# One-core transformer block kernel: vector sums reordered inside the block pairs of the up product, a four-pair TensorE loop, two down tiles computed by half contractions

## What is computed

```python
D_FF = 3 * D_MODEL                       # 3072
h = rms_norm(x, g_ffn_pre)
up = h @ w_up                            # (1024, 6144)
gate_h = causal_dwconv(up[..., :D_FF], ffn_conv_w, ffn_conv_b)   # 3 taps over tokens
hid = jax.nn.gelu(gate_h) * up[..., D_FF:]
x = x + rms_norm(hid @ w_down, g_ffn_post)
```

## Time and profile before

| | us |
|---|---|
| median of three runs | 3272.5 (3272.47 to 3274.01) |
| the profiled execution, its own time | 3272.96 |
| its span, first to last instruction | 3271.2 |
| PE busy in it | 3088.3 (94%) |
| DVE busy in it | 2314.0 (71%) |

### The profile page before, as it was taken

How to read it: one execution, slowest core, us unless ns; L and a number is a source line. 1 busy time by engine, 2 the same in 40 slices (tenths; PEclk the granted TensorE clock), 3 DMA queues, 4 the chain that set the end, 5 groups by cost and what they waited for, 6 DMA issues and landing times.

```text
span 3271.2 us, 44920 instructions
## 1 busy us (share of the span) xinstructions
PE 3088.3 (94%) x14885; PEld 2455.6 (75%) x14885; DVE 2314.0 (71%) x2995; ACT 1473.5 (45%) x2003; POOL 981.6 (30%) x511
## 2 busy tenths in 40 slices
PE   6999998888998799999969999999989999999998
PEld 5668776566786688888857888888767777778867
DVE  7788967886545899999966775633588888811266
ACT  4345433667222788888841366201443343300142
POOL 2224342000341011111104433345234444434432
PEclk8999999999998899999989999999999999999999
DMA  7223221340242999999972222134133333454312
GB/s 263 71 63 93 65 65 52 110 120 30 81 160 85 378 382 379 380 382 382 352 267 60 64 83 87 41 120 145 64 91 104 114 103 108 155 206 148 115 33 71
DMA packets 365271, 496.54 MB, mean 152 GB/s; under 512 B 34478, under 2 KB 237148, under 8 KB 365156
## 3 DMA queue, kind: packets, MB, share of 16 engines
q1 hardware_dynamic: 350356, 460.39, 41.0%
q10 hardware_dynamic: 5440, 17.86, 1.7%
q0 software_dynamic: 9360, 16.80, 1.4%
HBM read 422.57 MB, written 83.92 MB: 155 GB/s over the span
## 4 chain that ended last, share of the span: by engine, by line
PE 43%; DVE 13%; issue 4%; SPq 3%; DMA 2%; ACT 2%; DVEq 0%; POOL 0%; ACTq 0%; POOLq 0%
PE acc L450 9%; PE acc L451 9%; PE acc L452 9%; PE acc L2049 3%; PE acc L2051 3%; PE acc L2050 3%; DVE TT L3064 3%; PE acc L2068 1%; PE acc L2070 1%; PE acc L2069 1%; DVE UWL L2817 1%; SPq L1952 1%; DVE uu L3070 1%; DVE TT L3073 1%; DMA mraw<-in_exp_w 1%
## 5 line engine op out<-in xcount | busy, mean ns | idle before, releaser
L421 POOL TENSOR_TENSOR whi<-wraw,one 128x1024 fp32r<-128x1024 f32 (+1 forms) x153 | 289.9, 1895 | 1312.2 <-PE acc L452 1014.4
L450 PE MATMUL acc<-Ah,whi 128*128 128x512 f32 (+1 forms) x1568 | 620.3, 396 | 4.6 <-POOL wlo L423 3.2
L452 PE MATMUL acc<-Ah,wlo 128*128 128x512 f32 (+1 forms) x1568 | 611.0, 390 | 0.0
L451 PE MATMUL acc<-Al,whi 128*128 128x512 f32 (+1 forms) x1568 | 611.0, 390 | 0.0
L423 POOL TENSOR_TENSOR wlo<-wraw,whi 128x1024 fp32r<-128x1024 f32 (+1 forms) x153 | 381.5, 2493 | 12.0
L450 PEld LDWEIGHTS acc<-Ah,whi 128*128 128x128 f32 (+1 forms) x1568 | 294.2, 188 | 81.5 <-issue 18.9
L451 PEld LDWEIGHTS acc<-Al,whi 128*128 128x128 f32 (+1 forms) x1568 | 294.4, 188 | 63.6 <-issue 3.1
L452 PEld LDWEIGHTS acc<-Ah,wlo 128*128 128x128 f32 (+1 forms) x1568 | 294.2, 188 | 62.6
L2162 DVE TENSOR_TENSOR mlo<-mraw,mhi 128x1024 fp32r<-128x1024 f32 x256 | 306.9, 1222 | 37.5 <-ACT mhi L2106 23.8
L2106 ACT ACTIVATE mhi<-mraw 128x1024 fp32r<-128x1024 f32 x256 | 267.8, 1063 | 74.5 <-PE acc L2051 51.6
L2049 PE MATMUL acc<-mhi,XTh 128*128 128x512 f32 x512 | 203.8, 398 | 3.6 <-DVE XTl L2157 3.3
(11 more groups left out here) (726 smaller groups left out, 6651.0 us busy)
## 6 DMA issues: line engine op xcount, KB each, us to landing
mraw<-in_exp_w SPq DMA_DIRECT2D x512, 256.0 KB
mraw<-in_exp_w SPq DMA_DIRECT2D x128, 512.0 KB, 12.1
wraw<-in_w_in SPq DMA_DIRECT2D x72, 512.0 KB, 3.8
TT<-in_ada_w SPq DMA_DIRECT2D x32, 512.0 KB, 3.8
TT<-gates SPq DMA_DIRECT2D x32, 512.0 KB, 4.6
wraw<-in_w_up SPq DMA_DIRECT2D x24, 512.0 KB, 4.7
hidTh<-hidh SPq DMA_DIRECT2D x24, 512.0 KB, 2.6
hidTl<-TT SPq DMA_DIRECT2D x24, 512.0 KB, 3.6
```

Source lines behind the costliest of these rows:

```text
L421: ch(pool.tensor_tensor(hi[:, r, 0:k, 0:m], wraw[:, r, 0:k, 0:m], one[:, 0:1].unsqueeze(2).broadcast_to([P, k, m]), ALU.mult))
L450: pe.matmul(o, hi[:, hr, j, 0:m], ih[:, k0 + j, cols], start=(j == 0), stop=False)
L451: pe.matmul(o, hi[:, hr, j, 0:m], il[:, k0 + j, cols], start=False, stop=False)
L452: last = pe.matmul(o, lo[:, hr, j, 0:m], ih[:, k0 + j, cols], start=False, stop=(j == k - 1))
```

## The change

It has four edits. (1) In the loop and in pair 22, DVE does `result_e` ahead of the low part of weight 0, `result_f` ahead of that of weight 1, and `result_22` ahead of step 2. (2) Around pair 1, the first three sums of pair 1 stand between the readings of the second plain pair's banks, and the rest of the plain pairs' hidden tiles (step 2 of tile 0, the convolution of tile 1) behind them; the third sum goes to `uf` in place and is copied to `uu` later; step 2 of tile 1 goes to the end. On ACT `conv_first(1)` stands ahead of `hidden_high(0)`. (3) PE's loop holds four pairs and runs five times. (4) The two down tiles are computed in the order tile 0 with k = 0 to 3, tile 1 with k = 0 to 3, tile 0 with k = 4 to 7, tile 1 with k = 4 to 7, and the wait for the second tile's weights and bank stands in front of the second tile.

```diff
@@ ACT
+        conv_first(act, 1, 0, 32)
         hidden_high(act, 0, 1)
-        conv_first(act, 1, 0, 32)
         gelu(act, 1, 0)
@@ DVE, around pair 1
         weight_low(dve, 1, 5, 1, True)
-        second_half(0, 1, 2)
...
         dve.wait_ge(S("t_lo"), 16)
+        result_e(1, 1)
         ch(dve.tensor_tensor(ug[:], XX[:], R5, ALU.mult))
         dve.sem_inc(S("ug"), 1)
-        result_e(1, 1)
+        result_f(1, 1)
         ch(dve.tensor_tensor(uu[:], Y[:], R5, ALU.mult))
         dve.sem_inc(S("up_done"), 1)
+        dve.wait_ge(S("u_mid"), 3 + 2)
+        dve.wait_ge(S("u_used"), 7 + 4)
+        dve.tensor_tensor(uf[:], UBANKS[1][3], uf[:], ALU.add).then_inc(S("u_mid"), 1)
+        second_half(0, 1, 2)
         conv(1, 0)
-        result_f(1, 1)
         weight_low(dve, 2, 0, 0)
         second_half(1, 0, 1)
-        result_22(1, 1)
+        dve.wait_ge(S("u_mid"), 3 + 3)
+        ch(dve.tensor_copy(uu[:, hi_tok], uf[:]))
         for i in (1, 2):
             weight_low(dve, 2, i, 0)
-        second_half(1, 0, 2)
         result_11(1, 1)
...
         result_21(1, 1)
+        second_half(1, 0, 2)
@@ DVE, pair(n, p)
             conv(n, 1 - p)
+            result_e(n, p)
             if weights:
                 weight_low(dve, n + 1, 0, 1 - p)
-            result_e(n, p)
+            result_f(n, p)
             if weights:
                 weight_low(dve, n + 1, 1, 1 - p)
             second_half(n, 1 - p, 1)
-            result_f(n, p)
             if weights:
                 weight_low(dve, n + 1, 2, 1 - p)
+            result_22(n, p)
             second_half(n, 1 - p, 2)
-            result_22(n, p)
@@ PE
-        with pe.Fori(0, (BLOCKS - 2) // 2) as i:
+        with pe.Fori(0, (BLOCKS - 2) // 4) as i:
+            for r in range(4):
+                pair(4 * i + 2 + r, r % 2)
...
     def product_two(pe, n, ih, il):
+        for part in range(2):
             for r in range(2):
+                if part == 0:
+                    pe.wait_ge(w_lo, n + r + 1)
+                    pe.wait_ge(acc_free[r], take(r))
+                for j in range(4 * part, 4 * part + 4):
+                    if j % 2 == 0:
+                        pe.wait_ge(S(f"hid_in0_{j // 2}"), 64)
...
```

More of the change, by code:

```diff
@@ L3308, in _ @@
         pair(1, 1, tuple(("t_lo", 4 * q) for q in range(4)))
-        with pe.Fori(0, (BLOCKS - 2) // 2) as i:
-            for r in range(2):
-                pair(2 * i + 2 + r, r)
+        with pe.Fori(0, (BLOCKS - 2) // 4) as i:
+            for r in range(4):
+                pair(4 * i + 2 + r, r % 2)
         pair(BLOCKS, 0)
     def product_two(pe, n, ih, il):
[L3316 to L3321, removed]
-            for r in range(2):
[L3323 to L3328, removed]
+        for part in range(2):
+            for r in range(2):
+                if part == 0:
[4 more added lines that the diff above has]
+                        pe.wait_ge(S(f"hid_in0_{j // 2}"), 64)
+                    for h in range(2):
+                        o = acc[r][:, tokens(h)]
+                        pe.matmul(o, whi[:, r, j, :], ih[:, j, tokens(h)], start=(j == 0), stop=False)
+                        pe.matmul(o, whi[:, r, j, :], il[:, j, tokens(h)], start=False, stop=False)
+                        last = pe.matmul(o, wlo[:, r, j, :], ih[:, j, tokens(h)], start=False, stop=(j == KD - 1))
+                if part:
                     last.then_inc(w_used, 1)
```

## The result

Six executions of the changed kernel took 3302.84 us in the median (3299.74 to 3304.21), against 3274.02 us (3272.47 to 3276.75, six runs) for the kernel before on the same chip: a ratio of 1.0086, 95% interval 1.0074 to 1.0098, or 28 us slower. The median lies 15 us above the forecast of 3287.5 us and just beyond the upper end of the range; 1.5 us of that is the kernel before itself, which came out at 3274.0 in these six runs and at 3272.5 in the three from which the forecast started.

The account below looks back on a forecast made before the run. DVE was taken to pace the loop, with PE following. The terms +4.5 + 13.0 - 1.1 - 1.6 = +14.8 on 3272.96 gave 3287.8, stated as 3287.5 us since the median is 0.5 lower; range 3275 to 3302.

Parts of the forecast that it names:

- What bounds the kernel: In the loop of block pairs DVE sets the pace and PE follows, with 0.73 us a pair to spare.
- The order, 20 x 0.65 = +13.0: Loop pairs 2 to 21: the second sum, free in the gap before, costs DVE 0.65 us a pair, +13.0 in all.
- two effects oppose: In the pairs: the first sum hides a POOL operation, while POOL, released earlier, meets DVE's SBUF-only instructions; net 0.
- one meeting of 0.78: In the pairs: each overlap of POOL's work with DVE's taps or low parts costs DVE about 0.78 us.
- Shorter taps and low parts: Sign in the loop: the forecast is wrong if DVE's taps or low parts get shorter.
- POOL takes more: Rival in the loop: one more POOL meeting in each pair, 1.4 us a pair, 3302; chance 0.19.
- Behind the gap, third sum and step 2 only change places: In each pair, behind the gap after step 1: this swap was given no cost to DVE.
- The start, +4.5: Around pair 1: later step 2 of tile 0 delays SP's store and pair 2's weights; DVE enters the loop 4.5 late.
- The end of the loop, -1.1: At pair 22, which goes at PE's pace: the third sum comes earlier for part 6, -1.1 once.
- The down tiles, -1.6: Down product: PE starts 1.3 us earlier, stalls inside tile 0, no wait ahead of tile 2; -1.6.
- PE's longer loop, 0: PE's loop of four pairs: PE's spacing unchanged and PE has spare time anyway, so 0.
- my fourth rival: PE's longer loop stalls: an instruction fetch at each of four jumps back, up to +8, 3295; chance 0.05.

Follow-up runs that it names:

- third_early: The kernel before with only the third sum moved ahead of step 2 in the pairs; 3275.13 us, ratio 1.0004.
- second_early: The kernel before with only the second sum moved ahead of step 1 in the pairs; 3287.44 us, ratio 1.0037.
- order_only: The kernel before with only the new order of DVE's sums in the loop and in pair 22; 3300.84 us, ratio 1.0078.
- third_late: order_only with the third sum alone put back behind step 2; 3277.17 us, ratio 1.0008 to the kernel before.
- second_third: The kernel before with the second sum ahead of step 1 and the third ahead of step 2, first sum unmoved; 3305.50 us, ratio 1.0094.
- start_only: The kernel before with only the edits around pair 1, DVE's and ACT's; 3279.74 us, ratio 1.0014.
- step_kept: The kernel before with pair 1's sums moved early, but step 2 of tile 0 left ahead of them and ACT's order kept; 3275.48 us, ratio 1.0004.
- down_only: The kernel before with only the two down tiles by half contractions; 3272.92 us, ratio 0.9995.
- loop4_only: The kernel before with only PE's loop of four pairs; 3274.23 us, ratio 1.0001.
- gap_filled: The kernel before with the third sum moved right behind the second, into the idle gap behind step 1; 3268.59 us, ratio 0.9985.
- first_early: The kernel before with only the first sum moved ahead of the low part of weight 0; 3272.72 us, ratio 0.9994.

## Why the prediction was wrong

The sign was right and the mechanism half of it; the time was 15 us off. The largest part, 10.8 us, lies in one term.

**What bounds the kernel** held. DVE paces the loop: third_early gives PE its third sum 1.1 us earlier in every pair, and the iteration stays 39.60.

**The order, 20 x 0.65 = +13.0**, is the step that failed: "I take 0.65, no meeting gained or lost, as two effects oppose." Measured were +23.8 over 19 pairs, 1.25 each and 1.40 in the steady part. The 0.65 itself was right, as the price of the second sum out of the gap (second_early, 0.60). Both opposing effects exist as well, and the first sum's does give 0.25 to 0.60 back. But they don't cancel: the other one is 1.4 us a pair (order_only against third_late). I had written that POOL's last low part would start "on top of DVE's SBUF-only instructions instead of its last sum", and let it cancel against one meeting of 0.78. It hits two instructions at 1.1 each, repaid in part where POOL is done earlier: low parts of weight 0 and 1, a tap and a step 0 get shorter by 1.5 us a pair, against 2.2 for the two. Shorter taps and low parts were on my list of what would show the forecast wrong. The rest of the 1.40 is idle time, 0.87 us a pair, most of it the gap. The rival **POOL takes more** (3302) is what happened, with its place (`scaled_12`) and one instruction more.

What I could have read from the trace: I had POOL released earlier, but compared its start with no instruction of DVE's. The chain from third sum to POOL (4.5 us) and that from third sum to the low part of weight 5 (3.4 us, and 1.1 more once step 2 stands behind the sum) were both in the trace of before. Their difference of 1.07 us less 1.14 is below zero, and that decides, as long as PE waits for the third sum, which it does when the second is early (second_third, order_only) and not when it isn't (third_early).

**"Behind the gap, third sum and step 2 only change places"** sounds free, and alone it is (third_early). With the second sum early it costs 1.04 us a pair (second_third, 1.64, against 0.60 in second_early), and 1.40 beside the early first sum.

**The start, +4.5**: +4.6 by start_only, with SP's queue behind step 2 as its main cause (step_kept); 5.4 in the trace of start_only and 6.0 in the changed kernel's, where the order in pair 2 adds to it. The mechanism was right and the size within the bounds, in part by luck: the step was shorter than I had it, the landing longer, and the copy wasn't the equal of the sum that it replaces.

**The end of the loop, -1.1**: right. From step 1 of pair 21 to DVE's last step 0 it is 28.34 us before, 27.21 after and 27.20 in order_only. From the third sum of pair 21, which moved by as much, it is 23.68 us in all three: behind that sum PE sets the pace, as forecast. What I had left out stands behind it: PE's first down matmul follows 0.40 us behind that step before and 1.24 in order_only, as it waits for POOL's second split. The half contractions take this wait out of the changed kernel.

**The down tiles, -1.6**: by the median -1.6 alone, within the noise, and -1.9 us of span from the last step 0 (419.2 in order_only, 417.28 after). Against the kernel before (416.75) it is no gain in the trace, nor is down_only (416.67); order_only, down_only and the changed kernel have one stretch at half clock there and the kernel before none, so such differences of 1 to 2 us depend on the clock of one execution. Start 1.4 us earlier, stall inside tile 0, no wait ahead of tile 2: all as described. In the traces tile 2 comes 1.0 us later after all: there are three waits inside tiles 0 and 1 (0.66, 0.56 and 2.10 us) where I had one, and what follows the last ran at half clock for 3.4 us, which costs 1.5. PE in order of time:

```profile
2897.36 0.50 PE L3330 MATMUL acc<-Ah,whi 128*128 128x512 f32 x1 [2.10 <-DMA Al<-hidTl]
```

Busy time and granted clock (last but two) by stretch:

```profile
2898.00:2900.00 2.00, 2.00 (x8) 1.54 (x7) 0.00 (x0) 0.00 (x0) 0.00 (x0) 0.64 1.07 368
2900.00:2902.00 2.00, 2.00 (x6) 1.60 (x5) 0.11 (x1) 0.00 (x0) 0.06 (x1) 0.51 1.07 400
```

Six matmuls start in the second row's 2 us, 0.427 us apart; at 0.227 us each nearly nine would. My sum had no such term.

**PE's longer loop, 0**: right, by loop4_only. The Trainium skill ("Runtime: NRT & Kernel Launch", section on instruction fetch) gives TensorE an instruction memory of 128 KiB or 2048 instructions, and the trace agrees: a body of some 710 is not fetched again at its jumps back. What the same section says of jumps out of the window, which I had beside my fourth rival, showed no cost here.

## What to carry to other kernels

When a loop is paced by one engine, moving an instruction in its order costs what it costs there plus what it does to the neighbours whose port it shares. So for each moved release follow the chain to the moment at which the neighbour starts, and compare that with the moment at which the first instruction that can collide with it starts. The sign of the difference decided here and not the count of meetings: with POOL 0.06 us ahead of DVE's instruction (order_only) DVE's got 1.09 us longer, with POOL 0.07 us behind one (third_early) DVE's kept its length.

Moves that cost 0.60 us and nothing alone cost 1.64 us a pair together (second_third), so test pairs of moves where they act on the same release. Before an instruction is used as an anchor between two traces, make sure that the change leaves it where it was. And an idle gap of the pacing engine is worth filling with the next instruction that is ready (the third sum here, -0.44 us a pair) before it is worth emptying.

## What the runs showed of the hardware

- A meeting of DVE and POOL on SBUF-only instructions costs by turns, not by halves. In the changed kernel DVE's low part (0.69 us alone) lasts to 2566.59, 0.56 behind the end of POOL's at 2566.03, and POOL's next, from 2565.99, to 2567.72. So the cost is the rest of the neighbour's instruction: 1.1 us here, against the 0.78 that I had taken from the earlier trace rows. Where DVE's scaled sum started 0.07 us ahead of POOL (third_early), it kept its 0.69 and POOL's instruction took 1.77 us. The Trainium skill ("SBUF — State Buffer", section on two separate sides) calls the shared port pair an exclusive lock, and the trace agrees: in both cases the one that starts second is held up and the first isn't, and the second sum, which reads PSUM, takes 0.68 to 0.69 in every order.
- POOL's own busy time falls where it meets DVE's low part and scaled sum: 17.2 us busy in an iteration of the changed kernel, 18.97 in one of third_late and 18.95 before.
- The length of a stall didn't tell whether TensorE's clock fell. In the changed kernel a stall of 2.10 us was followed by 3.4 us at a granted clock of 0.5 (1.2 GHz of 2.4), from 1.2 us behind the stall's end; the stalls of 0.66 and 0.56 us ahead of it were not. But the stall of 3.17 us ahead of tile 2, the same in all kernels with the old down tiles, was followed by full clock in before, third_early, loop4_only, start_only and step_kept, and by half clock in gap_filled, order_only, second_third, second_early, third_late and first_early.
